# Shifted copies of the Conformer convolution: who starts them, and seven of them as engine copies

## The reference, cut to what matters

```python
def causal_dwconv(u, hist, w):
    ext = jnp.concatenate([hist.astype(u.dtype), u], axis=1)
    y = lax.conv_general_dilated(ext, w[:, None, :], window_strides=(1,), padding='VALID',
                                 feature_group_count=u.shape[-1])
    return y, ext[:, ext.shape[1] - (w.shape[0] - 1):]

def conformer_conv(x, hist, norm_g, w_pw1, b_pw1, conv_w, conv_b, ln_g, ln_b, w_pw2):
    a, g = jnp.split(rmsnorm(x, norm_g) @ w_pw1 + b_pw1, 2, axis=-1)
    u = a * jax.nn.sigmoid(g)
    y, new_hist = causal_dwconv(u, hist, conv_w)       # width 31, one filter per channel
    y = layernorm(y + conv_b, ln_g, ln_b)
    return jax.nn.silu(y) @ w_pw2, new_hist
```

## Time and profile before

| | us |
|---|---|
| median of 3 runs | 1467.84 |
| span of the profiled execution | 1461.8 |
| TensorE busy in it | 1395.3 (95%) |
| VectorE busy | 720.4 (49%) |
| ScalarE busy | 479.2 (33%) |
| GpSimd busy | 596.9 (41%) |

### The profile page before, as it was taken

How to read it: one execution, slowest core, us unless ns; L and a number is a source line. 1 busy time by engine, 2 the same in 40 slices (tenths; PEclk the granted TensorE clock), 3 DMA queues, 4 the chain that set the end, 5 groups by cost and what they waited for, 6 DMA issues and landing times.

```text
span 1461.8 us, 34670 instructions
## 1 busy us (share of the span) xinstructions
PE 1395.3 (95%) x14005; PEld 1299.8 (89%) x14005; DVE 720.4 (49%) x1256; ACT 479.2 (33%) x706; POOL 596.9 (41%) x329
## 2 busy tenths in 40 slices
PE   6998998988999999999999999988999999999998
PEld 5896767767999999999999977757999999999998
DVE  5646888874535443024442376667365430144411
ACT  4375333322333222222223321227433321222221
POOL 3322333322426554445543364422255554355441
PEclk9999999999999999999999999999999999999999
DMA  6417899979323222333312566542223323332122
GB/s 185 130 54 243 296 327 322 366 270 307 94 64 96 86 79 87 94 89 90 90 57 69 143 164 157 148 115 60 69 87 90 90 76 90 101 87 86 54 84 74
DMA packets 246246, 192.56 MB, mean 132 GB/s; under 512 B 12129, under 2 KB 205106, under 8 KB 246058
## 3 DMA queue, kind: packets, MB, share of 16 engines
q1 hardware_dynamic: 244561, 188.31, 41.9%
q10 hardware_dynamic: 1181, 1.44, 0.4%
q0 software_dynamic: 400, 1.32, 0.3%
HBM read 173.03 MB, written 6.04 MB: 122 GB/s over the span
## 4 chain that ended last, share of the span: by engine, by line
PE 74%; DVE 3%; issue 2%; ACT 1%; DMA 0%; POOL 0%; SPq 0%; ACTq 0%; DVEq 0%; POOLq 0%
PE banks L1810 64%; PE banks L2243 2%; PE banks L2076 2%; PE banks L1827 1%; PE banks L2015 1%; PE banks L1957 1%; PE banks L2192 1%; DMA u_sh<-u 0%; DVE k_grp L1300 0%; SPq L610 0%; ACTq L1106 0%; PE banks L2048 0%; PE banks L1965 0%; PE banks L2246 0%; DVE sb L1363 0%
## 5 line engine op out<-in xcount | busy, mean ns | idle before, releaser
L683 POOL TENSOR_TENSOR w_l<-w_raw,w_h 128x1024 fp32r<-128x1024 f32 (+2 forms) x195 | 439.3, 2255 | 411.9 <-ACT w_h L830 397.1
L1810 PE MATMUL banks<-xa_h,w_h 128*128 128x272 f32 x1856 | 388.1, 290 | 4.4 <-DVE tmp L1633 3.3
L1810 PE MATMUL banks<-xa_h,w_l 128*128 128x272 f32 x1856 | 385.2, 289 | 0.0
L1810 PE MATMUL banks<-xa_l,w_h 128*128 128x272 f32 x1856 | 383.6, 288 | 0.0
L1810 PEld LDWEIGHTS banks<-xa_h,w_h 128*128 128x128 f32 x1856 | 292.9, 189 | 6.7 <-issue 5.5
L1810 PEld LDWEIGHTS banks<-xa_l,w_h 128*128 128x128 f32 x1856 | 292.3, 189 | 0.0
L1810 PEld LDWEIGHTS banks<-xa_h,w_l 128*128 128x128 f32 x1856 | 290.4, 189 | 0.0
L830 ACT ACTIVATE w_h<-w_raw 128x1024 fp32r<-128x1024 f32 (+2 forms) x193 | 185.1, 961 | 200.2 <-PE banks L1810 199.9
L1810 PE MATMUL banks<-h_h,w_h 128*128 128x272 f32 x928 | 193.1, 289 | 0.3 <-DVE x L1572 0.3
L1810 PE MATMUL banks<-h_h,w_l 128*128 128x272 f32 x928 | 192.6, 289 | 0.0
L1810 PE MATMUL banks<-h_l,w_h 128*128 128x272 f32 x928 | 191.9, 288 | 0.0
(11 more groups left out here) (302 smaller groups left out, 1650.8 us busy)
## 6 DMA issues: line engine op xcount, KB each, us to landing
w_raw<-in_w_up SPq DMA_DIRECT2D x88, 512.0 KB, 3.7
k_grp<-in_cache_k SPq DMA_DIRECT2D x128, 256.0 KB, 4.4
v_pg<-in_cache_v SPq DMA_DIRECT2D x120, 256.0 KB, 5.1
w_raw<-in_w_in SPq DMA_DIRECT2D x24, 512.0 KB, 6.4
w_raw<-in_w_down SPq DMA_DIRECT2D x32, 384.0 KB, 3.1
w_raw<-in_w_pw SPq DMA_DIRECT2D x24, 512.0 KB, 3.7
w_raw<-in_w_down SPq DMA_DIRECT2D x32, 320.0 KB, 3.0
w_raw<-in_w_out SPq DMA_DIRECT2D x8, 512.0 KB, 5.6
```

The costliest lines, as they stand in the source:

```text
L683: g.tensor_tensor(w_l[:, slot, 0:n], w_raw[:, slot, 0:n], w_h[:, slot, 0:n].bitcast(F32), ALU.subtract).then_inc(s_lo, 1)
L1810: ins = mm(out[:, half, 0:HT], w, v[:, half * HT:(half + 1) * HT], start=first and t == 0 and n == 0, stop=last and t == phase.tiles - 1 a ...
```

## The change

SyncE starts only the copies with r = 0 and r = 1, 8 per chunk, and 3 of them for an edge chunk. GpSimd starts those with r = 3 and r = 2 for every chunk, 8 per chunk (inside its loop too, with the chunk number in a register), and 6 for an edge chunk: r = 3, and two of r = 1. ScalarE starts none any more: for the edge chunks it makes the four copies with r = 2 itself, as Copy instructions of 32 partitions. VectorE makes the three copies with r = 0, q = 0 to 2 of the edge chunks itself, ahead of `combine` and of the taps. GpSimd still makes every low part; its DMAs stand behind `tap_weights` of the same chunk, so they are ahead of the next low parts, which before had nothing ahead of them.

```diff
         SyncE, shifted(c)
-                for r, q in [(r, q) for r in range(4) for q in range(4)][:6 if c in (0, DC - 1) else 16]:
+                for r, q in [(r, q) for r in range(2) for q in range(4)][slice(3, 6) if c in (0, DC - 1) else slice(8)]:
                         sp.dma_start(u_sh[b][32 * r:32 * r + 32, q, r:TE], u[32 * q:32 * q + 32, c, 0:TE - r])\
                           .then_inc(s_ush[b], 16)
         GpSimd
-            def shifted_also(c):
+            def shifted_also(c, b):
...
+                edge = isinstance(c, int) and c in (0, DC - 1)
+                pool.wait_ge(s_u, c * 2 + 2)
...
+                if not (isinstance(c, int) and c < 2):
                     pool.wait_ge(s_cvp, c - 1)
-                for q in range(4):
-                    g.dma_start(u_sh[b][96:P, q, 3:TE], u[32 * q:32 * q + 32, c, 0:TE - 3]).then_inc(s_ush3, 16)
+                for r, q in [(r, q) for r in (3, 2) for q in range(4)] if not edge else [(3, q) for q in range(4)] + [(1, 2), (1, 3)]:
+                    g.dma_start(u_sh[b][32 * r:32 * r + 32, q, r:TE],
+                                u[32 * q:32 * q + 32, ds(c, 1), 0:TE - r].rearrange("p a t -> p (a t)")).then_inc(s_ushp[b], 16)
             def turn(i, last):
                 for j in range(4):
-                    if last and j == 2:
-                        for late in (2, 3):
-                            ahead(split_low, ph["pw1"], i, late, last)
-                        tap_weights(i * 2 + 1, 1)
-                        shifted_also(DC - 1)
-                    if last and j >= 2:
-                        continue
                     ahead(split_low, ph["pw1"], i, j, last)
                     if j % 2:
                         tap_weights(i * 2 + j // 2, j // 2)
-                        if isinstance(i, int) and i == 0 and j == 1:
-                            shifted_also(0)
+                        shifted_also(i * 2 + j // 2, j // 2)
         ScalarE, shifted_too(c)
-                for r, q in [(2, q) for q in range(4)] + [(1, 2), (1, 3)]:
-                        nc.scalar.dma_start(u_sh[b][32 * r:32 * r + 32, q, r:TE], u[32 * q:32 * q + 32, c, 0:TE - r])\
-                          .then_inc(s_ush[b], 16)
+                for q in range(4):
+                    A(u_sh[b][64:96, q, 2:TE], u[32 * q:32 * q + 32, c, 0:TE - 2], ACT.Copy).then_inc(s_ushc, 1)
         VectorE, chunk(i, b)
                 dve.wait_ge(s_u, c * 2 + 2)
+                if known and c in (0, DC - 1):
+                    for q in range(3):
+                        V.tensor_copy(u_sh[b][0:32, q, 0:TE], u[32 * q:32 * q + 32, c, 0:TE]).then_inc(s_ushc, 1)
         TensorE, pe_conv(c, b, n)
-                pe.wait_ge(s_ush[b], n * 256 + (192 if b == 0 or edge else 256))
+                pe.wait_ge(s_ush[b], n * 128 + (48 if b == 0 or edge else 128))
+                pe.wait_ge(s_ushp[b], n * 128 + (96 if b == 0 or edge else 128))
                 if edge:
-                    pe.wait_ge(s_ush3, 64 if c == 0 else 128)
+                    pe.wait_ge(s_ushc, 7 if c == 0 else 14)
```

More of the change, by code:

```diff
@@ L346, in build @@
         s_ush = [sem(f"u_shifted{n}") for n in range(2)]
-        s_ush3 = sem("u_shifted_by_three")
+        s_ushp, s_ushc = [sem(f"u_shifted_too{n}") for n in range(2)], sem("u_shifted_copied")
         s_tr, s_ev, s_sp, s_bk, s_sc, s_sev = (sem(n) for n in (
@@ L777, in tap_weights @@
                                 .to_broadcast([P, 32, 32]), ALU.mult).then_inc(s_wsh, 1)
-            def shifted_also(c):
-                b = c % 2
-                pool.wait_ge(s_u, 2 * c + 2)
-                if c == 0:
+            def shifted_also(c, b):
+                edge = isinstance(c, int) and c in (0, DC - 1)
+                pool.wait_ge(s_u, c * 2 + 2)
+                if isinstance(c, int) and c == 0:
                     pool.wait_ge(s_cz, 4)
-                else:
+                if not (isinstance(c, int) and c < 2):
                     pool.wait_ge(s_cvp, c - 1)
-                for q in range(4):
-                    g.dma_start(u_sh[b][96:P, q, 3:TE], u[32 * q:32 * q + 32, c, 0:TE - 3]).then_inc(s_ush3, 16)
+                for r, q in [(r, q) for r in (3, 2) for q in range(4)] if not edge else [(3, q) for q in range(4)] + [(1, 2), (1, 3)]:
+                    g.dma_start(u_sh[b][32 * r:32 * r + 32, q, r:TE],
+                                u[32 * q:32 * q + 32, ds(c, 1), 0:TE - r].rearrange("p a t -> p (a t)")).then_inc(s_ushp[b], 16)
             def turn(i, last):
                 for j in range(4):
-                    if last and j == 2:
-                        for late in (2, 3):
-                            ahead(split_low, ph["pw1"], i, late, last)
-                        tap_weights(i * 2 + 1, 1)
-                        shifted_also(DC - 1)
-                    if last and j >= 2:
-                        continue
                     ahead(split_low, ph["pw1"], i, j, last)
```

## The result

| | before | changed kernel |
|---|---|---|
| median, us | 1467.4 (4 runs) | 1480.08 (4 runs, 1475.8 to 1484.09) |
| span of the profiled execution, us | 1461.8 | 1474.1 |
| from u of chunk 0 to the first matmul of `pw2`, us | 146.94 | 160.05 |

The ratio is 1.0086 (95%: 1.0062 to 1.0109). The forecast was 1463.3, so it has the wrong sign. The stage of the convolution accounts for the whole loss: 160.05 - 146.94 = 13.1 us of stage against 12.3 us of span.

The account below looks back on a forecast made before the run. TensorE, busy 95% of the span, was taken as the bound, so copies win only where it waits. 2.5 + 1.6 + 0.4 + 0 = 4.5 us off the 1461.8 span gave 1457.3, plus 6.0 made 1463.3; range 1461.0 to 1467.8.

Parts of the forecast that it names:

- Chunk 0's wait and clock: Before and in chunk 0's convolution: 2.5 us of TensorE's 3.11 us copy wait won, 1.6 of 1.70 us slow clock regained.
- the sum had 4.1: The forecast's two chunk 0 terms: 2.5 us of wait and 1.6 us of slow clock.
- The durations: Chunk 0's work: SyncE's three starts 2.0 to 3.4 us, ScalarE's copies 0.86 each, VectorE's from 0.47 each, GpSimd's six starts 3.3.
- rival 1: At the edges engine copies hold GpSimd, so TensorE's wait hardly shrinks: about 1467 us, no telling difference; chance 0.16.
- the 3.1 us that the prediction quoted: The skill's measured time, where 0.62 us was usual, for GpSimd-begun DMAs whose descriptors wait during VectorE's fp32 SBUF copy.
- ScalarE comes free 2.7 us sooner: At chunk 0, four copies of 3.4 us replace 6.17 us of DMA issue, so ScalarE is done at 851.7.
- Inner chunks, "I take 0; ends -2 to 0": Chunks 1 to 6: moving eight starts to GpSimd was taken to change nothing, at worst losing 2 us.
- a low part stands still while the taps run: Inner chunks: GpSimd's low part waits for VectorE's taps, at most 7.8 us, read from one low part of 3.67 us.
- The starts of 4.0 us: Inner chunks: GpSimd's eight starts, 0.50 us each, can lie beside the taps, leaving GpSimd just full.
- Rival 2: GpSimd becomes the inner chunks' bound if loop starts cost over 1.3 us each; at 1.6, 1477 us; chance 0.13.
- Chunk 7, +0.4: At chunk 7, 0.4 us won, ends -1.2 to +0.45, from TensorE's 0.45 us wait.

Follow-up runs that it names:

- edges_alone: Kernel before, with only the edge chunks as in the changed kernel and the inner chunks keeping 16 starts on SyncE; 1470.64 us, ratio 1.002.
- starts_behind_low: Changed kernel, but in chunks 1 to 6 GpSimd makes the next low part first and begins its eight copies behind it; 1467.33 us, ratio 1.0015.
- behind_and_hold: starts_behind_low plus the wait of hold_chunk0; 1475.67 us, ratio 1.0058.
- inner_alone: Kernel before, with only the inner chunks changed: copies split 8 and 8 between SyncE and GpSimd; 1482.8 us, ratio 1.0101.
- hold_chunk0: Changed kernel, but GpSimd holds slab 5's low part until VectorE has done chunk 0's taps and scaled chunk 1's first half; 1478.36 us, ratio 1.0081.
- lows_after_taps: Changed kernel, but GpSimd holds each chunk's next low part until VectorE has scaled the next chunk's first half; 1467.76 us, ratio 1.0002.
- wait_only: Kernel before plus one wait: from chunk 1 GpSimd holds the first low part until VectorE has combined the chunk before; 1477.34 us, ratio 1.0067.

## Why the prediction was wrong, step by step

- **Chunk 0's wait and clock: right, and better than said.** 0.6 us of the wait were to stay, none did: `pe_conv(0)` starts 6.4 us behind u, where the slabs alone took 6.5 in the kernel before. It was narrow, since GpSimd's last copy landed at 853.75 and the convolution starts at 853.99. And the convolution ran at 1.00, 854 to 859, as forecast (5.0 for 6.70 us). From u to `pe_conv(0)` 3.2 us were won, from u to its end 3.2 + 1.7 = 4.9; the sum had 4.1.
- **The durations: right.** ScalarE's copies 0.853 us each (0.86 said), GpSimd's six starts 3.53 us (3.3), SyncE's three 1.92 (2.0 to 3.4); GpSimd's last copy landed 2.3 us behind the end of the last start (1.5 to 3.3). VectorE's copies 0.556 us instead of 0.47. The hold of rival 1 exists but is small: GpSimd's first start took 0.98 us beside the copies, where it took 0.69 before and 0.50 is the median. The rule of the Trainium skill (SBUF — State Buffer, section "SBUF: two separate sides") that such a copy keeps GpSimd from writing descriptors bears on this start above all (the second took 0.59); the 3.1 us that the prediction quoted were not seen, and VectorE's three copies took 1.73 us in all.
- **"ScalarE comes free 2.7 us sooner": right, and its result missed.** It is done with them 3.8 us behind u (851.39) instead of 6.5 (854.75), so the low parts of the next slabs start at 852.52 instead of 855.88. That is no gain, it is a collision: 3.60 us of wait of TensorE at 862.56 and 1.9 us more between `pe_conv(0)` and `pe_conv(1)`. I asked what a later engine costs and not what an earlier one runs into.
- **Inner chunks, "I take 0; ends -2 to 0": this step failed.** The contention was seen, and with the right partner, but one row was taken for a rule. From 906.64/910.31 I concluded that "a low part stands still while the taps run". That row shows a low part that arrives during the ninth of eleven taps (they are those of chunk 3, not 4), and in the kernel before all six inner low parts arrive at the ninth or tenth. The other outcome was in the rows too: VectorE's L1702, 0.25 us when undisturbed, was held to 1.83 us. The starts of 4.0 us were booked as harmless filling, yet they also decide when the next low part arrives: directly behind u and the sum, in the first taps, where the tap is the one that stands still, 5.9 to 7.1 us per chunk. The lower bound had to be the other side of the same row: if the taps wait, VectorE's 72.5 of 108 us grow by 6.6 us a chunk, 11.5 + 6.6 = 18.1 us against 17.2. That is 5 us over the six chunks, and worth a rival of its own; the waits measured in the inner chunks are 5.9 us, and the slow clock behind two of them adds 3.4.
- **Rival 2 had the sign and not the mechanism.** Its starts cost 0.497 us in the loop, register or not, longest 0.977 against its limit of 1.3. GpSimd isn't what TensorE waits for; VectorE is. That its 1477 us came near the 1480 measured is luck.
- **Chunk 7, +0.4:** with the taps free it gave 1.9 us (edges_alone, starts_behind_low); in the changed kernel it lost 6.1, because u and the sum came late and TensorE waited 8.0 us for the sum.

Two points stay open. In the changed kernel the row of GpSimd meets the taps as one long hold in some chunks and takes turns with them in others, and the waits of TensorE fall in three of five intervals; why these, no run shows.

The other is the spread: edges_alone, starts_behind_low and behind_and_hold lie 15 to 21 us apart between runs, the kernel before 7 to 11 us in each of its sets. A part of that lies outside the change. Ahead of the stage the 13 kernels with a trace do the same work (but for two early weights of GpSimd in two of them), and yet u of chunk 0 is ready at times from 846.9 us (edges_alone) to 857.7 us (inner_alone). The late ones had the slower clock: up to there TensorE's clock stood at 0.50 for 13.7 us in the kernel before, the changed kernel, edges_alone and hold_chunk0 (846.9 to 849.9 us), for 23.9 us in those with u ready at 851.4 to 854.0 us, and for 34.1 us in inner_alone. Behind the first matmul of `pw2` all lie within 1.4 us. The runs without a trace agree in the main: of 23 runs of the kernel before beside lows_after_taps the fastest (1461.84 us) had a mean granted clock of 0.989, the slowest (1471.64 us) 0.983. So the stage column says more than medians that lie a few us apart. But not all of the spread is that: the slowest run of starts_behind_low (1482.08 us) had 0.987, and with the stage of its trace, 161.1 us, behind_and_hold couldn't have run in its 1467.62 us, so the stage differs between executions as well. That a low part near the border below falls now on one side and now on the other would explain it, but only one execution of each has a trace; it is argued, not shown.

## What to carry to other kernels

When two engines contend for operations that read SBUF, price both outcomes: the one who waits may change when either moves by a few microseconds. Anything put in a queue, here 4 us of DMA starts that themselves were free, moves all that stands behind it, so mark in the trace what the moved work will lie beside. And before a new distribution of work is called bad, hold the displaced operation with one wait: here that alone took back 12.4 of 12.7 us.

## What the runs showed of the hardware that was not expected

- **Who goes first depends on when the low part arrives.** Over the traces of all these kernels, a low part of GpSimd that did not follow directly on another of its operations and arrived during one of the first six of a chunk's 11 taps went ahead within 0.6 us and a tap stood still, some 50 cases (852.52, 869.36 and 871.42 above are three). One that arrived at the seventh tap or later waited until the last tap was done, 33 of 34 cases (889.09, 896.66 and the earlier trace rows), up to 2.9 us; the exception is 876.81 of wait_only, at the seventh tap. The Trainium skill (SBUF — State Buffer, section "SBUF: two separate sides") says of the shared port that it is an exclusive lock for a whole instruction and that whoever starts first has it. These rows agree that one of the two stands still and does not merely slow down; they add that a row of operations of one engine can keep the other out over several of them: four taps ahead of a low part, or three GpSimd operations over one tap of 7.76 us. Why the sixth tap is the border no run shows.
- **Two forms of the same collision.** The three GpSimd operations cost VectorE 2.14 + 2.12 + 1.66 = 5.9 us when they take turns with taps, and 7.05 us when one tap waits for all.
- **A DMA start of GpSimd loses nothing beside VectorE's two-input fp32 operations and a little beside one-input ones.** The traces hold 572 such starts of copies. Of 382 that lay beside VectorE's work, but beside no copy and no one-input tap, the median is 0.498 us and the longest 0.53. All 70 that took over 0.56 us lay beside a copy into `u_sh` or one of a chunk's first two taps, which have one SBUF input; the longest took 0.98 us, and 113 others lay beside such an operation without loss. Of the eight starts from 865.16, 4.19 us, seven take 0.50 to 0.52 us and the one beside these taps (867.15) 0.73.
